# Two units of a fused two-layer kernel multiplied ahead of the norm's factor, and per-token scaling on GpSimd

## The reference

```python
mod = c_act @ w_ada + b_ada
shift, scale, gate = jnp.split(mod, 3, axis=-1)
h = rms_norm_2(x, g) * (1.0 + scale[:, None]) + shift[:, None]
proj = jnp.einsum('bsd,df->bsf', h, w_in)          # 2048 -> 7168 columns
...
out = jnp.einsum('bsf,fd->bsd', y, w_out)
return x + gate[:, None] * out
# rms_norm_2(x, g) = x * rsqrt(mean(x*x over features) + eps) * g
```

## Time and profile before

| | us |
|---|---|
| median of 3 runs | 1532.18 (1531.68 to 1532.27) |
| profiled execution, its time | 1532.22 |
| profiled execution, its span | 1530.6 |
| TensorE busy | 1517.0 (99%) |
| VectorE busy | 1135.4 (74%) |
| ScalarE busy | 778.5 (51%) |
| GpSimd busy | 32.1 (2%) |
| granted TensorE clock, mean | 0.995 of full |

### The profile page before, as it was taken

One profiled execution on the slowest core, in us unless ns is written; L12 is line 12 of the kernel. 1 busy time (PEld: TensorE's weight loads), 2 busy tenths in 40 slices (PEclk: granted clock), 3 DMA queues, 4 the chain that ended last, 5 costly groups with the idle time before them and its releaser, 6 DMA issues. The chain is left out here.

```text
span 1530.6 us, 32029 instructions
## 1 busy us (share of the span) xinstructions
PE 1517.0 (99%) x12558; PEld 1479.0 (97%) x12558; DVE 1135.4 (74%) x1373; ACT 778.5 (51%) x931; POOL 32.1 (2%) x60
## 2 busy tenths in 40 slices
PE   9999999999999999999999999999999999999997
PEld 8999997999999999999999999999999989999997
DVE  7878777668997878878788887879854644764754
ACT  7645456546454445444444444445554644454544
POOL 0000000000000000000000000000000000000000
PEclk9999999999999999999999999999999999999998
DMA  9574556557886867767676776866475554555551
GB/s 343 177 275 161 199 198 210 184 180 261 309 307 222 302 221 273 267 232 285 238 272 241 261 272 221 300 224 214 141 255 194 196 193 160 161 164 179 163 182 56
DMA packets 86428, 340.29 MB, mean 222 GB/s; under 512 B 9784, under 2 KB 10320, under 8 KB 79824
## 3 DMA queue, kind: packets, MB, share of 16 engines
q1 hardware_dynamic: 77904, 281.05, 53.0%
q0 software_dynamic: 7584, 55.61, 10.3%
q10 hardware_dynamic: 864, 2.53, 0.4%
HBM read 337.02 MB, written 2.13 MB: 222 GB/s over the span
## 5 line engine op out<-in xcount | busy, mean ns | idle before, releaser
L720 DVE TENSOR_TENSOR wlo<-raw,whi 128x1024 fp32r<-128x1024 f32 x528 | 643.1, 1223 | 338.2 <-ACT whi L349 334.5
L349 ACT ACTIVATE whi<-raw 128x1024 fp32r<-128x1024 f32 x527 | 556.8, 1060 | 634.0 <-PE PS L1364 565.3
L1360 PE MATMUL PS<-gh,whi 128*128 128x256 f32 x3056 | 847.8, 277 | 0.0
L1364 PE MATMUL PS<-gh,wlo 128*128 128x256 f32 x3056 | 841.3, 275 | 0.0
L1362 PE MATMUL PS<-gl,whi 128*128 128x256 f32 x3056 | 841.2, 275 | 0.0
L1360 PEld LDWEIGHTS PS<-gh,whi 128*128 128x128 f32 x3056 | 573.8, 188 | 4.0 <-DVE wlo L720 1.8
L1362 PEld LDWEIGHTS PS<-gl,whi 128*128 128x128 f32 x3056 | 573.8, 188 | 0.8
L1364 PEld LDWEIGHTS PS<-gh,wlo 128*128 128x128 f32 x3056 | 573.7, 188 | 0.0
L1360 PE MATMUL PS<-ah,whi 128*128 128x256 f32 x688 | 189.2, 275 | 0.0
L1362 PE MATMUL PS<-al,whi 128*128 128x256 f32 x688 | 189.2, 275 | 0.0
L1364 PE MATMUL PS<-ah,wlo 128*128 128x256 f32 x688 | 189.2, 275 | 0.0
(11 more groups left out here) (256 smaller groups left out, 926.3 us busy)
## 6 DMA issues: line engine op xcount, KB each, us to landing
raw<-weights SPq DMA_DIRECT2D x527, 512.0 KB, 3.6
ada_w<-w_ada POOLq DMA_DIRECT2D x48, 1024.0 KB, 6.3
EM<-rows POOLq DMA_DIRECT2D x1, 3072.0 KB, 13.9
X<-xT SPq DMA_DIRECT2D x3, 512.0 KB, 8.8
c<-const ACTq DMA_DIRECT2D x1, 1536.0 KB, 6.8
c_act<-c_rows POOLq DMA_DIRECT2D x1, 1024.0 KB, 6.8
KF<-rows POOLq DMA_DIRECT2D x2, 512.0 KB, 5.9
outT<-X SPq DMA_DIRECT2D x2, 512.0 KB, 3.1
```

The source lines that it names most:

```text
L349: act.activation(whi[:, j % SPLIT, first:first + 1024], raw[:, j, :], ACT.Copy).then_inc(s_hi, 1)
L720: dve.tensor_tensor(wlo[:, j % SPLIT, first:first + 1024], raw[:, j, :], whi[:, j % SPLIT, first:first + 1024].bitcast(F32), ALU.subtract) ...
L1360: pe.matmul(out[:, t, :], whi[:, b, w], hi[:, kt, :], start=first and half == 0 and (apart or t % 2 == 0), stop=False, skip_group_check=True)
L1364: mm = pe.matmul(out[:, t, :], wlo[:, b, w], hi[:, kt, :], start=False, stop=last and half == 1, skip_group_check=True)
```

## The change

The first two units of the second mixer are multiplied by features without the factor. `RXH` and `RXL` (in the space of CV, ah and al) hold X * gain of tiles 0 to 3 in two parts, and 2 more columns with the shift; rows are 258 columns. `product_raw` puts unit 0 right behind `last_pair` into banks 4 to 7, each output tile once VectorE has read it out (`s_tile`); then comes the column sum, which is one source now since VectorE adds all four squared tiles with `near`; then unit 1, with the spread of the factor (`column_turn`) behind its first 12 matmuls. Units 2 to 7 of group 0 take tiles 4 to 15 (`NORMED` gives the order, tiles 0 to 3 come last and serve from group 1 on). For the first 4 of the 16 tiles in that order VectorE writes TH as before (two from PSUM, two from `rb`, which ScalarE copies from PSUM ahead of the second gh); for the other 12 GpSimd does, in two instructions with a wait between them. GpSimd also takes the sum of the squares of X tiles 0 to 7. VectorE's tile adds stand ahead of its folds. VectorE evicts group 0 in slots 6 and 7: own * rb, plus the shift's column, plus the rest of the group. `column_squares` is divided in `column_sums` and `column_turn`, also where the last norm uses it, with the same order of work there. The cut diff (the placement of RXH and RXL, declarations, `product_high_first`, which goes, and changed counts are left out):

```diff
-        TURNS = (3, 5, 7, 9, 11, 13, 15)
+        TURNS = (1, 3, 5, 7, 9, 11)
+        NORMED = tuple(range(4, DT)) + tuple(range(4))
...
+            pool.wait_ge(s_sq, SQUARES[2] + 2)
+            pool.tensor_tensor(SQX2[:, 0, :, :], SQX2[:, 0, :, :], SQX2[:, 1, :, :], ALU.add).then_inc(s_sum, 1)
+            pool.wait_ge(s_copy, 1)
+            for n in range(4, DT):
+                t = NORMED[n]
+                if n >= 8:
+                    pool.wait_ge(s_gl, 2 * DT + 10 + n - 7)
+                pool.tensor_tensor(TH[:, n % 8, :], X[:, t, :], rb[:, :], ALU.mult).then_inc(s_hq, 1)
+                pool.wait_ge(s_hq, n - 3)
+                pool.tensor_scalar(TH[:, n % 8, :], TH[:, n % 8, :], modT[:, 16 + t:17 + t], None, ALU.mult).then_inc(s_hp, 1)
             pool.wait_ge(s_gain, 4)
-            pool.wait_ge(s_copy, 1)
+            pool.wait_ge(s_copy, 2)
...
+                if d == 1:
+                    act.wait_ge(s_mt, 1)
+                    act.activation(RXH[:, :, S:S + 2], modT[:, 0:4].unsqueeze(2).to_broadcast([P, 4, 2]), ACT.Copy
+                                   ).then_inc(s_rxh, 1)
+                    for t in range(4):
+                        act.activation(RXH[:, t, 0:S], X[:, t, :], ACT.Copy, scale=modT[:, 16 + t:17 + t]).then_inc(s_rxh, 1)
...
+            split(B_IN2 - 1, LEAD + 6)
             column_root(2)
-            for t in range(DT):
-                act.wait_ge(s_h, t + 1)
-                act.activation(gh[:, t, :], TH[:, t % 8, :], ACT.Identity, bias=modT[:, t:t + 1]).then_inc(s_gh, 1)
-                if t in TURNS:
-                    split(B_IN2 - 1, LEAD + 6 + TURNS.index(t))
+            for n, t in enumerate(NORMED):
+                if n == 1:
+                    act.wait_ge(s_h, 2)
+                    act.activation(rb[:, :], spread(2), ACT.Copy).then_inc(s_copy, 1)
+                if n < 4:
+                    act.wait_ge(s_h, n + 1)
+                else:
+                    act.wait_ge(s_hp, n - 3)
+                act.activation(gh[:, t, :], TH[:, n % 8, :], ACT.Identity, bias=modT[:, t:t + 1]).then_inc(s_gh, 1)
+                if n in TURNS:
+                    split(B_IN2 - 1, LEAD + 7 + TURNS.index(n))
...
+                    if g == 1:
+                        act.wait_ge(s_evac, G_IN2 + 3)
...
+                    dve.wait_ge(s_rxh, 1)
+                    dve.wait_ge(s_mt, 1)
+                    dve.tensor_tensor(RXL[:, :, S:S + 2], modT[:, 0:4].unsqueeze(2).to_broadcast([P, 4, 2]),
+                                      RXH[:, :, S:S + 2].bitcast(F32), ALU.subtract).then_inc(s_rxl, 1)
+                    for t in range(4):
+                        dve.wait_ge(s_rxh, t + 2)
+                        dve.scalar_tensor_tensor(RXL[:, t, 0:S], X[:, t, :], modT[:, 16 + t:17 + t],
+                                                 RXH[:, t, 0:S].bitcast(F32), ALU.mult, ALU.subtract).then_inc(s_rxl, 1)
...
             split(B_IN2 - 1, LEAD + 4)
-            sum_chunk(2, 1, SQX2)
             add_to_x(8 * (B_IN2 - 1) + 5, G_IN2 - 2, (G_IN2 - 2) % 2, 8)
-            fold(2, 1, SQX2)
             last_add(0)
+            dve.wait_ge(s_sum, SUMS[2] + 1)
+            link(dve.tensor_tensor(SQX2[:, 0, 0:2, :], SQX2[:, 0, 0:2, :], SQX2[:, 0, 2:4, :], ALU.add))
+            last_add(1)
+            dve.tensor_tensor(SQX2[:, 0, 0, :], SQX2[:, 0, 0, :], SQX2[:, 0, 1, :], ALU.add).then_inc(s_fold, 1)
             dve.wait_ge(s_sq, SQUARES[2] + 3)
             link(dve.tensor_tensor(SQX2[:, 1, 0:2, :], SQX2[:, 1, 0:2, :], SQX2[:, 1, 2:4, :], ALU.add))
-            last_add(1)
-            dve.tensor_tensor(SQX2[:, 1, 0, :], SQX2[:, 1, 0, :], SQX2[:, 1, 1, :], ALU.add).then_inc(s_dve, 1)
-            links[0] += 1
             last_add(2)
-            dve.wait_ge(s_dve, links[0])
+            link(dve.tensor_tensor(SQX2[:, 1, 0, :], SQX2[:, 1, 0, :], SQX2[:, 1, 1, :], ALU.add))
             dve.wait_ge(s_fold, 3)
             dve.tensor_tensor(SQX2[:, 0, 0, :], SQX2[:, 0, 0, :], SQX2[:, 1, 0, :], ALU.add).then_inc(s_near, 1)
-            near(2, 0, SQX2, 1)
             last_add(3)
+            for t in range(4):
+                near(2, t, SQX2, 1 + t)
             dve.wait_ge(s_tile, 4)
             dve.sem_inc(s_evac, 1)
             split(B_IN2 - 1, LEAD + 5)
 
-            dve.wait_ge(s_mt, 1)
             dve.wait_ge(s_rcol, 1)
             dve.reciprocal(rcol[:, 0, :], rcol[:, 0, :]).then_inc(s_icol, 1)
+            split(B_IN2 - 1, LEAD + 6)
             dve.wait_ge(s_spread, 1)
-            for t in range(DT + 1):
-                if t < DT:
-                    if t >= 8:
-                        dve.wait_ge(s_gl, 2 * DT + 10 + t - 7)
-                    dve.scalar_tensor_tensor(TH[:, t % 8, :], X[:, t, :], modT[:, 16 + t:17 + t], spread(2),
+            for n in range(2):
+                t = NORMED[n]
+                dve.scalar_tensor_tensor(TH[:, n % 8, :], X[:, t, :], modT[:, 16 + t:17 + t], spread(2),
+                                         ALU.mult, ALU.mult).then_inc(s_h, 1)
+            for n in range(1, DT + 1):
+                if n in (2, 3):
+                    t = NORMED[n]
+                    if n == 2:
+                        dve.wait_ge(s_copy, 1)
+                    dve.scalar_tensor_tensor(TH[:, n, :], X[:, t, :], modT[:, 16 + t:17 + t], rb[:, :],
                                              ALU.mult, ALU.mult).then_inc(s_h, 1)
-                if t:
-                    k = t - 1
-                    dve.wait_ge(s_gh, 2 * DT + 6 + k + 1)
-                    dve.scalar_tensor_tensor(gl[:, k, :], TH[:, k % 8, :], modT[:, k:k + 1], gh[:, k, :].bitcast(F32),
-                                             ALU.add, ALU.subtract).then_inc(s_gl, 1)
-                    if k in TURNS:
-                        split(B_IN2 - 1, LEAD + 6 + TURNS.index(k))
+                k = NORMED[n - 1]
+                dve.wait_ge(s_gh, 2 * DT + 6 + n)
+                dve.scalar_tensor_tensor(gl[:, k, :], TH[:, (n - 1) % 8, :], modT[:, k:k + 1], gh[:, k, :].bitcast(F32),
+                                         ALU.add, ALU.subtract).then_inc(s_gl, 1)
+                if n - 1 in TURNS:
+                    split(B_IN2 - 1, LEAD + 7 + TURNS.index(n - 1))
+
+            def raw_out():
+
+                dve.wait_ge(s_used, 8 * B_IN2 + 2 + SPLIT)
+                dve.tensor_copy(shifted_part, PS[:, 4:8, S]).then_inc(s_raw_out, 1)
+                for t in range(4):
+                    dve.tensor_tensor(QB[:, t, :], own[:, t, :], rb[:, :], ALU.mult).then_inc(s_raw_out, 1)
+
+            def first_out():
+
+                dve.wait_ge(s_used, 8 * B_IN2 + 8 + SPLIT)
+                for t in range(4):
+                    dve.wait_ge(s_raw_out, t + 2)
+                    ins = dve.scalar_tensor_tensor(QB[:, t, :], acc_tiles(G_IN2 % 2)[:, t, :], shifted_part[:, t:t + 1],
+                                                   QB[:, t, :], ALU.add, ALU.add)
+                ins.then_inc(s_evac, 1)
...
+                if n == 6:
+                    raw_out()
+                if n == 7:
+                    first_out()
...
+            def product_raw(n):
+
+                unit = 8 * B_IN2 + n
+                if n == 0:
+                    pe.wait_ge(s_lo, unit + 1)
+                    for tiles in (range(3), (3,)):
+                        for kt in range(2):
+                            pe.wait_ge(s_rxl, kt + 2)
+                            for t in tiles:
+                                if kt == 0:
+                                    pe.wait_ge(s_tile, t + 1)
+                                out, w = raw_tile(kt, t)
+                                pe.matmul(out, whi[:, 0, w], RXH[:, kt, 0:S + 2], start=(kt == 0), stop=False,
+                                          skip_group_check=True)
+                                pe.matmul(out, whi[:, 0, w], RXL[:, kt, 0:S + 2], start=False, stop=False,
+                                          skip_group_check=True)
+                                mm = pe.matmul(out, wlo[:, 0, w], RXH[:, kt, 0:S + 2], start=False, stop=False,
+                                               skip_group_check=True)
+                    mm.then_inc(s_used, 1)
+                    column_sums(2, SQX2, (None,), 5)
+                    return
+                pe.wait_ge(s_hi, unit + 1)
+                pe.wait_ge(s_rxl, 5)
+                for kt in (2, 3):
+                    for t in range(4):
+                        out, w = raw_tile(kt, t)
+                        for x in (RXH, RXL):
+                            pe.matmul(out, whi[:, 1, w], x[:, kt, 0:S + 2], start=False, stop=False, skip_group_check=True)
+                        if (kt, t) == (3, 1):
+                            column_turn(2, (spread(2),))
+                pe.wait_ge(s_lo, unit + 1)
+                for kt in (2, 3):
+                    for t in range(4):
+                        out, w = raw_tile(kt, t)
```

(42 more changed lines are left out.)

18 lines of the change are left out of this document (10 added, 8 removed).

## The result

The changed kernel takes 1539.16 us (median of 6 runs, 1538.99 to 1540.17) against 1532.18 for the kernel before: a ratio of 1.0049, 95% interval 1.0038 to 1.0059. It is 7.0 us slower, where 1528.0 was forecast. Its profiled execution has a span of 1537.7 us, 7.1 more than before.

What follows compares the result with a forecast made beforehand. TensorE bounds the kernel, busy 1517.0 of 1530.6 us. Seam losses fall from 7.35 to 2.85 us, a gain of 4.5, less 0.3 for late tiles: 1532.2 - 4.2 = 1528.0 us, range 1526.3 to 1536.

Steps and rivals of the forecast that it cites:

- The seam: Between last down-projection unit and second mixer: 7.35 us lost before, 2.85 after, a gain of 4.5.
- rival C: The clock falls all the same in the wait, column sums and spread: 3 us, 1531.0; chance 0.08.
- GpSimd's sum: Squares' sum ahead of the first half-fold: 2.35 us, costing nothing, or up to 1.5 us if held up.
- Units 2 and 3: Second mixer: factor copy and unit 3's conversion delay tiles; waits of 0.6 and 0.2, unit 4 at 1103.3.
- The other 12 tiles: GpSimd's scaled tiles: 1.4 us each against 1.68 allowed, so it keeps ahead; 0.3 us off for small lateness.
- rival B: A GpSimd instruction of this size is dear by itself: 2.0 us a tile, 1531.5 to 1534; chance 0.13.
- rival A: GpSimd and VectorE hold each other up, tiles come 6.7 us late: 2.2 us slower, 1534.4; chance 0.27.
- Both signs: In units 5 to 9: VectorE's conversions longer than 1.23 us, or GpSimd's pairs more than 1.68 us apart.
- VectorE's relief: VectorE's work per pair of tiles falls from 3.15 us to about 2.2, below a unit's 2.72.

Runs made afterwards that it cites:

- e_ahead_sum: e_ahead with the sum of the squares back on VectorE in place of GpSimd; 1527.30 us.
- e_vector_scales: The changed kernel with all 16 scaled tiles written by VectorE again, the squares' sum staying on GpSimd; 1531.27 us.
- e_psum_no_gain: The changed kernel with seven VectorE conversions reading PSUM, a conversion turn added after tile 13, and GpSimd's second instruction left out; 1528.59 us.
- e_turn13: The changed kernel with one more conversion turn, after tile 13, so unit 9's weights are converted ahead of the last two tiles; 1535.78 us.
- e_ahead: e_vector_scales with unit 9's conversion behind tile 13 and each scaled tile written one place earlier (gl n, then TH n+2); 1527.03 us.

## Why the prediction was wrong

**The seam was right.** Without a factor unit 0 started at 1089.53, directly behind the last down unit. Its tile adds were in time, the third only just: it ended at 1090.15, where 1089.4 was forecast, and its first matmul is at 1090.24. TensorE waited 0.57 for the column sum (forecast 0.45), the spread took 0.36 to the next matmul (0.7), unit 2 started at 1097.52 (1097.0) with a wait of 0.29 (0.3), the clock stayed full; rival C did not happen. The one thing missed here is GpSimd's sum: at 3.86 us it held the first half-fold by 0.86, within the 1.5 that stood as its bound. About half of that reached TensorE, which started the column sum at 1093.21 where 1092.8 was forecast. e_ahead_sum shows that the sum on VectorE, at 1.13 us of its time, would have been no quicker.

**"Units 2 and 3"**: a wait of 0.6 was forecast, and it was 1.0, since TH 2 and TH 3 took 0.96 and 0.95 and the gl between them 0.69, each 0.48 in e_vector_scales. Unit 4 started at 1104.49, not 1103.3, so the lead was 3.35 us there and not 4.5. With nothing lost behind it that makes 1532.2 - 3.35 = 1528.85, and e_psum_no_gain, where nothing is, took 1528.59.

**The step that failed is "The other 12 tiles".** Its allowance of 1.68 us a tile was right, and its price, 1.4, was not; the 2.24 measured has two parts. The first is GpSimd's own, at most 1.82: the second instruction was put at 0.5, from "one input perhaps half of two", and costs 0.92 alone. The rows had no instruction of that form, and the range of 0.9 to 2.0 did hold it, so this was rival B with a milder size: it is worth (1.82 - 1.68) x 12 = 1.7 us, and taking the instruction away gave 1.6. Not all of it is price, since gl and TH tiles still meet GpSimd at that pace: at the 1.72 of the tile least held up it would be 0.5.

The second part is rival A, 0.42 us a tile: 5.0 us by the tiles' pace, 4.7 by the time. Both signs named for it came: conversions of 1.77 us, and GpSimd's pairs more than 1.68 apart. The forecast kept them as alternatives, with 0.27 and 0.13; they came together.

Rival A's sum took the two queues as wholly exclusive, and that is too much: with the measured prices it would have ended at 1097 + 13.6 + 12 x 1.65 = 1130.4, and the last gl ended at 1125.1. That rival A named 1125.0 is luck: its price of 1.2 us a tile was too low and its exclusion too strong. The rule of the Trainium skill (SBUF — State Buffer, "Who interferes with whom") that was weighed there holds in its condition, two SBUF inputs against a GpSimd instruction that reads SBUF, by 723 against 1598 ns and no change with an operand in PSUM. The page's "exclusive lock" is more than the 1.67 us for a pair of 1.14 and 0.72 show, and here the measurement decides.

**A cause that was not in the prediction: what stands behind the late tiles in the queues.** Unit 9's conversion is placed behind the sixteenth tile on ScalarE and VectorE. While tiles were expected in time this cost nothing, and so it wasn't costed. With late tiles unit 9 started 1.8 us behind the last gl, and the half clock behind that wait took 1.6 more; e_turn13 gave 3.4 back. That put the time past the range's upper end of 1536.

**VectorE's relief was partly lost.** Its pair was to fall from 3.15 to about 2.2 us. By its rows a conversion and two gl take 1.14 + 0.40 + 0.87 = 2.41, since one gl of the two is stretched, and the pair as a whole takes 4.41, waits for ScalarE included. And the lead needed no relief at all: e_ahead keeps it with all 16 tiles on VectorE.

## What to carry to other kernels

Work moved to an idle engine costs its price there, measured in the form and size used, and what it does to the engine that it helps. Where GpSimd's products meet VectorE's work on two SBUF operands, count their times nearly as one queue (1.67 of 1.86 us); beside its one-input form it is less (2.47 of 3.20), and there GpSimd bears most of it. Where an engine seems too slow by its pace, read what ends the idle time in front of its operations first: here 0.4 of 3.15 us were waits for another engine, and writing inputs one place earlier took them away at no cost. And a step that begins earlier takes away the cover of every engine that was only just in time behind it, so cost the stretch behind it at the new start.

## What was not expected of the hardware

A GpSimd tensor_scalar of 256 columns with a column as scalar (0.92 us) or a constant (0.85) takes longer than a product of two tensors (0.72), and that with the column broadcast as the second operand least of all (0.61). The form with one SBUF input also loses more beside VectorE's two-operand work (2.23 us) than the one with two (1.60), and slows VectorE less: VectorE's 1024-column operations took 1.21 and 1.41 in turn beside the former, 1.74 beside the latter.
